# A two-block model kernel on one core: the last two query tiles' chunks alternate, VectorE takes six first rows, GpSimd multiplies in four pieces, gate weights go by pairs

## What is computed

```python
def mlstm_inputs(q_raw, k_raw, v_raw, g_raw, conv_w, b_gate):   # g_raw = (h @ w_in)[..., OFF_G:], 16 gate columns
    ...
    g = (g_raw + b_gate).astype(jnp.float32).reshape(B, T, 2, 2, MLSTM_HEADS)
...
# the PEER feed-forward, per token: hf is the normed, modulated input (256 x 2048)
#   q      = hf @ wq                                  8 heads x 2 halves x 128 -> 2048 columns
#   scores = q . keys  (128 keys for each half)       top 16 of each half, 256 sums, top 16 of those
#   picked = 8 heads x 16 = 128 expert numbers, with softmax weights g
#   a      = gelu(hf . u[picked])                     128 rows of the table u, 2048 wide
#   out    = sum over picked of g * a * v[picked]     128 rows of the table v, 2048 wide
#   x_lat  = x_lat + m_lat[5] * out
```

## Time and profile before

| | us |
|---|---|
| median of three runs | 3043.69 (3042.84 to 3045.92) |
| the profiled execution | 3041.31, of which the span from first to last instruction is 3039.6 |
| DVE busy | 2464.4 (81% of the span) |
| PE busy | 2118.4 (70%) |
| ACT busy, POOL busy | 884.6 (29%), 652.6 (21%) |
| 16 DMA engines | 958.53 MB, mean 315 GB/s |
| chain that ended last | PE 57%, DMA 24%, DVE 13%, issue 3%, POOL 2%, ACT 1% |

### The profile page before, as it was taken

One profiled execution on the slowest core, in us unless ns is written; L12 is line 12 of the kernel. 1 busy time (PEld: TensorE's weight loads), 2 busy tenths in 40 slices (PEclk: granted clock), 3 DMA queues, 4 the chain that ended last, 5 costly groups with the idle time before them and its releaser, 6 DMA issues.

```text
span 3039.6 us, 24810 instructions
## 1 busy us (share of the span) xinstructions
PE 2118.4 (70%) x8610; PEld 1588.1 (52%) x8610; DVE 2464.4 (81%) x2631; ACT 884.6 (29%) x928; POOL 652.6 (21%) x656
## 2 busy tenths in 40 slices
PE   9999999999999999999999910004555200015653
PEld 7888888888888887788788810001222000002221
DVE  6675689999899987575566899979997899987677
ACT  5544443333333365534455311110000000000000
POOL 0000000000000000000000076773333343333332
PEclk9999999999999999999999955556777655557675
DMA  6454778888898965444354599999999999999997
GB/s 247 173 199 168 297 268 325 327 339 339 329 336 328 343 232 173 146 153 156 125 207 167 216 409 398 417 422 422 422 421 422 422 422 422 422 422 421 422 421 313
DMA packets 133193, 958.53 MB, mean 315 GB/s; under 512 B 14834, under 2 KB 15154, under 8 KB 17138
## 3 DMA queue, kind: packets, MB, share of 16 engines
q0 software_dynamic: 89824, 650.98, 52.7%
q1 hardware_dynamic: 43280, 306.44, 27.4%
q10 hardware_dynamic: 2, 0.01, 0.0%
HBM read 955.23 MB, written 2.13 MB: 315 GB/s over the span
## 4 chain that ended last, share of the span: by engine, by line
PE 57%; DMA 24%; DVE 13%; issue 3%; POOL 2%; ACT 1%; SPq 0%; DVEq 0%; POOLq 0%; ACTq 0%
DMA rows_g<-in_v_tab_dram,idx 18%; PE bank L645 17%; PE bank L649 17%; PE bank L646 17%; DVE rows_g L2661 9%; DMA rows_g<-in_u_tab_dram,idx 6%; PE bank L1186 2%; POOL rows_g L620 1%; DVE bank L2710 1%; DMA raw<-in_wstream_dram 1%; PE bank L679 1%; PE bank L1000 0%; PE bank L946 0%; PE bank L687 0%; PE bank L892 0%
## 5 line engine op out<-in xcount | busy, mean ns | idle before, releaser
L1806 DVE TENSOR_TENSOR WL<-raw,WH 128x2048 fp32r<-128x2048 f32 x287 | 656.8, 2290 | 290.5 <-ACT WH L1200 284.8
L1186 PE MATMUL bank<-rows_g,diag 128*128 128x512 f32 x488 | 362.0, 911 | 726.8 <-DMA rows_g<-in_v_tab_dram,idx 726.8
L645 PE MATMUL bank<-WH,UH 128*128 128x512 f32 x1952 | 770.4, 395 | 4.3 <-DVE WL L1806 2.8
L649 PE MATMUL bank<-WH,UL 128*128 128x512 f32 x1952 | 761.1, 390 | 0.0
L646 PE MATMUL bank<-WL,UH 128*128 128x512 f32 x1952 | 760.2, 389 | 0.0
L1200 ACT ACTIVATE WH<-raw 128x2048 fp32r<-128x2048 f32 x287 | 549.9, 1917 | 679.1 <-DMA raw<-in_wstream_dram 665.5
L1186 PEld LDWEIGHTS bank<-rows_g,diag 128*128 128x128 f32 x488 | 138.9, 299 | 950.4 <-issue 658.1
L2661 DVE CUSTOM_DVE_ANT_0 rows_g<-rows_g,bank 128x2048 f32<-128x2048 f32 x233 | 524.7, 2285 | 35.8 <-DMA rows_g<-in_u_tab_dram,idx 35.2
L2710 DVE SCALAR_TENSOR_TENSOR bank<-rows_g,gate_w,bank 128x2048 f32<-128x2048 f32 x193 | 454.6, 2355 | 116.3 <-DMA rows_g<-in_v_tab_dram,idx 97.8
L645 PEld LDWEIGHTS bank<-WH,UH 128*128 128x128 f32 x1952 | 366.9, 188 | 81.2 <-issue 4.1
L649 PEld LDWEIGHTS bank<-WH,UL 128*128 128x128 f32 x1952 | 366.8, 188 | 77.0
(11 more groups left out here) (410 smaller groups left out, 1629.6 us busy)
## 6 DMA issues: line engine op xcount, KB each, us to landing
raw<-in_wstream_dram SPq DMA_DIRECT2D x288, 1024.0 KB, 4.9
ada_w<-in_ada_dram POOLq DMA_DIRECT2D x96, 1024.0 KB, 7.4
rows_g<-in_u_tab_dram,idx POOLq DMA_INDIRECT x256, 23.8
rows_g<-in_v_tab_dram,idx POOLq DMA_INDIRECT x256, 30.0
X<-in_x_dram SPq DMA_DIRECT2D x4, 512.0 KB, 9.5
c_row<-in_c_rows_dram POOLq DMA_DIRECT2D x1, 2048.0 KB, 8.8
ctx_x<-in_ctx_dram POOLq DMA_DIRECT2D x1, 2048.0 KB, 11.2
gb<-mod_rows POOLq DMA_DIRECT2D x2, 1024.0 KB, 5.9
```

What stands on the lines that cost most here:

```text
L645: pe.matmul(o, ah[:, k0 + k, t], wh[:, w], start=first and k == 0, stop=False)
L649: mm = pe.matmul(o, al[:, k0 + k, t], wh[:, w], start=False, stop=last and k == nk - 1)
L1186: mm = pe.matmul(bank[c], diag[:, n % 2, :], row(q)[:, c * CW:(c + 1) * CW], start=s == mine[0], stop=s == mine[-1])
L1806: dve.tensor_tensor(WL[:, n % SLOTS_W, :], raw[:, n % SLOTS_W, :], WH[:, n % SLOTS_W, :].bitcast(F32), ALU.subtract).then_inc(lo_ready, 1)
```

## The change

1. **Query tiles 2 and 3.** Their eight chunks come in turn: chunk m of tile 2, chunk m of tile 3, and so on (`tile_pair`, and the stream is laid out to match). Both tiles are copied to `q_tok` after the last chunks, and their transposes and key products come behind all chunks. After four of the eight chunks the first halves of `UH` and `UL` (places 0 and 2) are no longer read.
2. **Places and first rows.** `ROW_AT` and `ROW_CHUNK` follow: places 14, 15 wait for no chunk, 0 and 2 for the fourth last chunk but one, then two places for each chunk, and 7, 11, 1, 3 for the last. Six first rows instead of three are dotted with `XN2` from SBUF, ahead of the copies of tiles 2 and 3. Row 3 goes from GpSimd to VectorE.
3. **Choices.** The last piece of `choose` (`idx`) is put to the piece ahead of it.
4. **GpSimd** multiplies a row in four instructions of 512 elements.
5. **Gates.** The high and the low part of the gate weights lie side by side (32 columns), so that 16 x 2 matmuls do what 16 x 3 did. The product low by low is now there as well. `both`, two identities under each other, adds the two halves in `gate_rows`. VectorE builds it once.

```diff
--- before.py
+++ after.py
@@ -68,9 +68,9 @@
 GATH = 14
-ROW_AT = (14, 15, 4, 8, 5, 9, 6, 10, 7, 11, 0, 1, 2, 3)
-ROW_CHUNK = (0, 0, 1, 1, 2, 2, 3, 3, 4, 4, 4, 4, 4, 4)
-FIRST_ROWS = 3
+ROW_AT = (14, 15, 0, 2, 4, 8, 5, 9, 6, 10, 7, 11, 1, 3)
+ROW_CHUNK = (None, None, 0, 0, 1, 1, 2, 2, 3, 3, 4, 4, 4, 4)
+FIRST_ROWS = 6
 SHARE = 4
@@ -203,7 +203,7 @@

-    return q < POOL_UNTIL and q % POOL_SHARE == POOL_SHARE // 2
+    return POOL_BEHIND <= q < POOL_UNTIL and q % POOL_SHARE == POOL_SHARE // 2

@@ -358,8 +358,8 @@

-        wg_h = [view("wg_h0", "P", 6656, [KT, NG], F32R), view("wg_h1", "TMP", 5136, [KT, NG], F32R)]
-        wg_l = [view("wg_l0", "P", 6912, [KT, NG], F32R), view("wg_l1", "TMP", 5136 + KT * NG, [KT, NG], F32R)]
+        wg_s = [view("wg_s0", "P", 6656, [KT, 2 * NG], F32R), view("wg_s1", "TMP", 5136, [KT, 2 * NG], F32R)]
+        wg_h, wg_l = [w[:, :, 0:NG] for w in wg_s], [w[:, :, NG:2 * NG] for w in wg_s]
         g_row = [view("g_row0", "P", 11272, [T]), view("g_row1", "TMP", 5136 + 2 * KT * NG, [T])]
@@ -435,6 +435,7 @@
         spare = tiny("spare", [1])
+        both = tiny("both", [NG])
         l_ms = [tiny(f"l_ms{i}", [NB * MH]) for i in range(3)]
@@ -602,7 +603,10 @@
                 pool.wait_ge(sem("xn2_ready"), 1)
-                pool.tensor_tensor(row(q), row(q), XN2[:, 0, :], ALU.mult).then_inc(sem("pool_made"), 1)
+                for c in range(D // CW):
+                    w = slice(c * CW, (c + 1) * CW)
+                    ins = pool.tensor_tensor(row(q)[:, w], row(q)[:, w], XN2[:, 0, w], ALU.mult)
+                ins.then_inc(sem("pool_made"), 1)

@@ -611,9 +615,10 @@
                     if q < GATH:
-                        if not ROW_CHUNK[q]:
+                        if ROW_CHUNK[q] is None:
                             pool.wait_ge(sem("xn2_ready"), NB)
-                        pool.wait_ge(split_used, NCH - SLOTS_W + ROW_CHUNK[q])
+                        else:
+                            pool.wait_ge(split_used, NCH - SLOTS_W + ROW_CHUNK[q])
                     else:
@@ -888,9 +893,9 @@
                 for k in range(KT):
-                    for j, (part, w) in enumerate(((UH, wg_h), (UH, wg_l), (UL, wg_h))):
-                        mm = pe.matmul(DB[2 + s][0:NG, 0:T], w[s][:, k, :], part[:, k, :], start=j == 0 and k == 0,
-                                       stop=j == 2 and k == KT - 1)
+                    for part in (UH, UL):
+                        mm = pe.matmul(DB[2 + s][0:2 * NG, 0:T], wg_s[s][:, k, :], part[:, k, :], start=part is UH and k == 0,
+                                       stop=part is UL and k == KT - 1)
                 mm.then_inc(sem("gate_ps"), 1)
@@ -898,7 +903,7 @@
                         g0 = (2 * d + typ) * MH
-                        mm = pe.matmul(DB[2 + typ][0:MH, d * T:(d + 1) * T], ident[0:NG, g0:g0 + MH], g_row[s][0:NG, :],
+                        mm = pe.matmul(DB[2 + typ][0:MH, d * T:(d + 1) * T], both[0:2 * NG, g0:g0 + MH], g_row[s][0:2 * NG, :],
                                        start=True, stop=True)
@@ -1125,6 +1130,17 @@

+            def tile_pair(n, q, work):
+                for m in range(CPT):
+                    for j in range(2):
+                        if m == 0:
+                            pe.wait_ge(acc_free_act, q + j + 1)
+                            pe.wait_ge(acc_free_dve, q + j + 1)
+                        products(n + 2 * m + j, ACC[(q + j) % 2], m * CK, CK, None, 0, UH, UL, first=m == 0, last=m == CPT - 1)
+                        next(work, None)
+                for _ in work:
+                    pass
+
             def queries_turned(r):
@@ -1148,11 +1164,11 @@
                 for t in range(OUT_TILES):
-                    yield from until(CPT * (t + 1))
+                    yield from until(CPT * (t + 1) if t < 2 else CPT * OUT_TILES)
                     pe.wait_ge(acc_free_act, Q_WQ + t + 3)
...
                     turn(lambda j, m: q_tok[:, t % 2, m % 2, (2 * j + m // 2) * P:(2 * j + m // 2 + 1) * P], DB[0:2], "pq_turned")
-                    yield from until(CPT * (t + 1) + 1)
+                    yield from until(CPT * (t + 1) + 1 if t < 2 else 0)
                     pe.wait_ge(sem("q_t_ready"), 2 * (t + 1))
@@ -1165,8 +1181,10 @@
             queries_turned(1)
-            linear_among(S_WQ, Q_WQ, 0, OUT_TILES, queries(), ready=u_parts(4, 1),
+            asked = queries()
+            linear_among(S_WQ, Q_WQ, 0, 2, islice(asked, 2 * CPT), ready=u_parts(4, 1),
                          each=lambda k: (sem("u_ready"), KT * 4 + k + 1))
+            tile_pair(S_WQ + 2 * CPT, Q_WQ + 2, asked)

@@ -1497,7 +1515,7 @@
                     seq.sync()
-                act.activation(wg_h[s][:, :, :], wg[:, :, :], ACT.Copy).then_inc(sem("wg_hi"), 1)
+                act.activation(wg_h[s], wg[:, :, :], ACT.Copy).then_inc(sem("wg_hi"), 1)

@@ -1725,19 +1743,28 @@
                 for t in range(OUT_TILES):
-                    yield from until(CPT * (t + 1) + 1)
+                    yield from until(CPT * (t + 1) + 1 if t < 2 else CPT * OUT_TILES)
                     for j in range(2):
...
                                        ACT.Copy).then_inc(sem("q_t_ready"), 1)
-                    yield from until(CPT * (t + 1) + 2)
+                    yield from until(CPT * (t + 1) + 2 if t < 2 else 0)
                     for b in range(NB):
...

-            linear_among(S_WQ, Q_WQ, 0, OUT_TILES, to_q, queries())
+            asked = queries()
+            linear_among(S_WQ, Q_WQ, 0, 2, to_q, islice(asked, 2 * CPT))
+            for m in range(2 * CPT):
+                hi(S_WQ + 2 * CPT + LEAD + m)
+                next(asked, None)
+            for t in (2, 3):
+                act.wait_ge(split_used, NCH + t - 3)
+                to_q((Q_WQ + t) % 2, t)
+            for _ in asked:
+                pass

@@ -2225,7 +2252,7 @@
                 dve.wait_ge(sem("gate_ps"), 2 * s + 1)
-                dve.tensor_copy(g_row[s][0:NG, :], DB[2 + s][0:NG, 0:T]).then_inc(sem("g_row_ready"), 1)
+                dve.tensor_copy(g_row[s][0:2 * NG, :], DB[2 + s][0:2 * NG, 0:T]).then_inc(sem("g_row_ready"), 1)

@@ -2322,10 +2349,11 @@
                 dve.wait_ge(sem("wg_hi"), s + 1)
-                dve.tensor_tensor(wg_l[s][:, :, :], wg[:, :, :], wg_h[s][:, :, :].bitcast(F32), ALU.subtract).then_inc(
+                dve.tensor_tensor(wg_l[s], wg[:, :, :], wg_h[s].bitcast(F32), ALU.subtract).then_inc(
                     sem("wg_ready"), 1)
...
             gate_weights(0)
+            link(dve.tensor_tensor(both[0:2 * NG, :], ident[0:2 * NG, 0:NG], ident[0:2 * NG, NG:2 * NG], ALU.add))

@@ -2577,12 +2605,6 @@
                     dve.wait_ge(sem("pq_turned"), 2 * (t - 1))
-                if t == OUT_TILES - 1:
-                    next(begun, None)
-                    for q in range(FIRST_ROWS):
-                        dot(0, q, XN2[:, 0, :])
-                    next(begun, None)
-                    dve.wait_ge(split_used, NCH)
                 dve.tensor_copy(q_tok[:, t % 2, 1, :], ACC[par][1][:, :]).then_inc(acc_free_dve, 1)
@@ -2629,12 +2651,14 @@
                     link(dve.tensor_reduce(exp_f[s][:, :], hots, AX.X, ALU.add))
-                    yield
+                    if s == 0:
+                        yield
                 link(dve.scalar_tensor_tensor(pick_f[:, :], exp_f[0][:, :], float(NKEY), exp_f[1][:, :], ALU.mult, ALU.add))
...
                 dve.tensor_copy(idx[:, b, mine], pick_f[:, :]).then_inc(sem("idx_ready"), 1)
+                yield

@@ -2663,7 +2687,16 @@
             linear_among(S_WQ, Q_WQ, 0, 2, to_q, islice(begun, 2 * CPT))
-            linear_among(S_WQ, Q_WQ, 2, OUT_TILES, to_q, islice(begun, 2 * CPT), work_first=True)
+            for m in range(2 * CPT):
+                next(begun, None)
+                lo(S_WQ + 2 * CPT + LEAD + m)
+            next(begun, None)
+            for q in range(FIRST_ROWS):
+                dot(0, q, XN2[:, 0, :])
+            next(begun, None)
+            for t in (2, 3):
+                dve.wait_ge(split_used, NCH + t - 3)
+                to_q((Q_WQ + t) % 2, t)

@@ -2824,7 +2857,9 @@
     put(S_OUT2, chunks(np.concatenate([mixed[D_SGU + D_ML:], mixed[:D_SGU + D_ML]])))
-    put(S_WQ, chunks(first["peer_wq_2"]))
+    asked = chunks(first["peer_wq_2"])
+    put(S_WQ, asked[:2])
+    put(S_WQ + 2 * CPT, asked[2:].swapaxes(0, 1))

```

## The result

| | before | changed |
|---|---|---|
| median | 3043.69 us | 3054.61 us (3050.17 to 3056.13, 7 runs) |
| ratio, changed to before | | 1.003, 95% interval 1.0021 to 1.0039 |
| profiled execution, span | 3041.31, 3039.6 | 3056.0, 3054.2 |

The change makes the kernel slower, by 9 to 11 us. The forecast was 3037.2, faster by 6.5, and the range ended at 3043.5.

A forecast was written before the change was run, and what follows sets the result against it. The prediction took the bound to be TensorE ahead of 1752 us, then how early VectorE hands back rows to the gathers. Its terms, -3.5 + 2 - 5 = -6.5 us, gave 3037.2 us, with an 8-in-10 range of 3031.5 to 3043.5.

The forecast's parts named there:

- What bounds the kernel: Gather stage: DMA engines lose time while VectorE hands back places too slowly; how early it hands back row 51 counts.
- The gates: Two blocks of gate matmuls on TensorE, 32 instead of 48 in each: -3.5 us, between -3.7 and -2.5.
- The first gathers: Before 1763 us: first gather at 1722.3 instead of 1729.84, 7.3 us of DMA lead, useful only if VectorE follows.
- the last rival: Early gathers share the engines with the last chunks, which reach TensorE late; at most 3 us lost; chance 0.05.
- VectorE to row 7: Head of the gather stage: row 7 done 0.5 to 3.5 us later than before; taken as +2 us.
- The half choice: VectorE's second half of a choice behind six dots: up to 3 us more if GpSimd's first multiplication meets it.
- The wait for the keys: VectorE's choice of group 2 waits for xn_ps, q_t, keys and score copy: 1.88, 1.07, 2.17 and 0.6 us.
- the list of signs: What the profile should show if right, such as VectorE idle some 3 us ahead of the choice of group 2.
- GpSimd in four pieces: Choices beside multiplications: shorter holds on VectorE, between 1.8 and 8.4 us saved; the middle, -5 us, taken.
- The rival in which the locks stay: GpSimd's quarters fall between VectorE's short instructions, each waiting again; 1.8 us saved, total 3040.4 to 3041.9; chance 0.28.
- The rival on the other side: Over 0.9 us fixed price per piece makes GpSimd the bound; at 1.5 us, some 3055 to 3070; chance 0.07.
- The sum: Gates -3.5, VectorE to row 7 +2, GpSimd in four pieces -5: -6.5 us in all, forecast 3037.2 us.

The follow-up runs named there:

- e4: The kernel before with only the gate part of the change (32 matmuls instead of 48 in each block); 3040.2 us, ratio 0.9989.
- e3: The changed kernel with VectorE's low part of the last chunk moved behind the two next pieces of the choice; 3044.1 us, 0.9997 of the kernel before.
- e11: The changed kernel with its first two gathers held back until TensorE has used the chunk the next two wait for; 3045.1 us, 0.9999 of before.
- e2: The changed kernel with VectorE's copies of tiles 2 and 3 moved ahead of the six first rows; 3046.4 us, 1.0007 of the kernel before.
- e7: The changed kernel with three first rows instead of six ahead of the copies of tiles 2 and 3; 3046.5 us, 1.0005 of the kernel before.
- e1: The changed kernel with GpSimd's multiplication of a row in one instruction again; 3050.4 us, 1.0020 of the kernel before.
- e5: The kernel before with only GpSimd's multiplications cut into four pieces, back to back; 3045.7 us, ratio 1.0006.
- e6: The changed kernel with each of GpSimd's four pieces waiting for the end of the one before; 3045.0 us, 0.9999 of the kernel before.
- e8: The changed kernel with one-instruction multiplication, last low part behind two choice pieces, copies behind two of six first rows; 3036.1 us, 0.9972 of the kernel before.
- e9: e8 with the multiplication in four pieces that each wait for the one before; 3031.3 us, 0.9955 of the kernel before.
- e10: The kernel before with only the multiplications cut into four pieces that each wait for the one before; 3042.0 us, ratio 0.9991.

## Why the prediction was wrong

**What bounds the kernel.** Right: the time follows how early VectorE hands back the rows up to the end of the choices, and the lead of the gathers was worth nothing without that.

**The gates.** Right: -3.5 forecast, -3.8 in the trace, -3.4 alone (e4).

**The first gathers.** Right in time, 1722.78 against 1729.84. Their lead was somewhat smaller than added up: from 1720 to 1763 the DMA engines moved 366 GB/s instead of 311, 2.4 MB more over 43 us, where 3.1 were forecast. That they cost something was the last rival, with 0.05, and it was put at the wrong place. It asked how late the chunk may come for **TensorE** ("a load of 15 us instead of 4.9"). The one that waited was VectorE, which stood for the low part with the six dots and the whole choice behind it. The step itself allowed "up to 2.5 more with gathers beside it"; the load took 4.9 more.

**VectorE to row 7.** +2 forecast, +11.7 in the two traces, 11.3 by the head. By the steps:
- The dots began at 1749.98 instead of 1744 to 1747: the forecast was 3 to 6 us too early, by the load (e3 and e11).
- The six dots took 13.3 us, as forecast.
- The half choice meets the multiplication: 5.4 us. It was named as "up to 3 us on top" and left out of the sum, since the multiplication should begin behind that piece. Its start, 1766.74, came even later than the 1763 forecast; but the piece ran until then as well, because the load had moved it. The bound of 3 was wrong too: it fits holds that begin 1.4 us into a multiplication, but an instruction that meets its start is held for all of it. Rows at hand showed this: the 4.50 us of 1757.97 begin with the multiplication of 4.52 at 1757.89, and the prediction only noted that this block would be gone.
- The wait for the keys: 5.86 us, against 1.88 + 1.07 + 2.17 + 0.6 = 5.7 forecast. This term was right, though the list of signs speaks of "some 3 us" for the same wait, which its own sum contradicts; e2 and e7 show that it was there only because of the order of the copies.

The rule of the Trainium skill (SBUF — State Buffer, "SBUF: two separate sides") that was weighed there says that a VectorE instruction with two SBUF inputs holds the ports only against a GpSimd instruction that reads SBUF. The issues did stay long: five beside the dots take 1.90 to 1.91 us. The prediction took this as speaking against the rule, which does not follow. An issue takes `idx` as its input, which lies in SBUF, and whether GpSimd reads it there no run shows. The rule had no part in the error.

**GpSimd in four pieces.** -5 forecast, +1.6 measured (e1, e5). This term is off by 6.6 us; that of row 7, with the load and the hold, is off by 9.3 to 9.7. The step that failed is "it would wait until the second piece ends". "No row shows which engine wins when both ask" was written beside it, and yet the middle of two gains was taken. The rival in which the locks stay was nearer, but its mechanism was not the one found: it had several short VectorE instructions wait for a piece each, while without a wait one instruction waits for all that is left (3.64 us for `pick_i`). What it describes happens in e6, with the wait. It too had only gains (-1.8), and no bound lay above zero, though four pieces make each multiplication 0.4 us longer. The size was right for another kernel: with a wait between the pieces the same stretch is 167.9 instead of 173.6 us, 5.7 shorter than before (e6).

**The rival on the other side**, a fixed price that makes GpSimd the bound, did not occur: a piece of 512 elements takes 1.27 us, and four 4.92, 0.4 more than one instruction of 2048, so 0.13 for each further piece.

**The sum** with the measured terms: -3.5 + 2 + 4.5 (the load, from the middle of the forecast's 1744 to 1747) + 5.4 (the hold) + 1.6 (the pieces) = +10.0, against 9 to 11 measured. Taken from the table it is 11.3 for the head, 1.6 for "to 79" and -3.8 for the gates, 9.1, and 10.8 with the rest named next.

Open is a small rest: from row 79 to row 98 the changed kernel takes 44.9 us and the one before 43.2, though no choice and no change lies there. e1, e2, e6, e7, e8, e9 and e11 take 44.3 to 45.3 too, e3 43.5. No run takes this apart.

## What to carry to other kernels

Ask of each transfer that starts earlier which transfer it now shares the engines with, and which engine stands waiting for that one with work behind it; move that work ahead of the wait. Cutting an instruction that blocks a neighbour into pieces does nothing as long as the pieces stand back to back: put a wait between them, and count the shorter hold only where the neighbour sets the pace (e9 against e10). An edit that moves a piece of work by 5 us can move it into another engine's long instruction, so price that meeting at its full length.
